# Experts' gate and up products on one Trainium2 core: weight blocks stationary instead of tokens

## The reference, cut to what matters

```
def _swiglu(h, wg, wu, wd):
    return (jax.nn.silu(h @ wg) * (h @ wu)) @ wd

top_val, top_idx = lax.top_k(logits, TOP_K)          # TOP_K = 2 of N_EXPERTS = 8
for e in range(N_EXPERTS):                           # wg, wu: 1024 x 3584, wd: 3584 x 1024
    out = out + combine[:, e:e + 1] * _swiglu(t, wg[e], wu[e], wd[e])
```

## Time and profile before

| | us |
|---|---|
| median of 3 runs | 1435.74 |
| lowest and highest | 1433.92, 1436.13 |
| the profiled execution's own time | 1435.94 |
| its span in the trace | 1434.3 |

### The profile page before, as it was taken

The page is one execution under the profiler, slowest core; times in us unless marked ns, Lnnn a source line. Parts: engine busy times, 40 slices in busy tenths (PEclk is TensorE's granted clock), DMA queues, the critical chain, the costliest instruction groups (busy, mean ns, idle before and its releaser), DMA issues.

```text
span 1434.3 us, 18278 instructions
## 1 busy us (share of the span) xinstructions
PE 1398.9 (98%) x6864; PEld 1136.0 (79%) x6864; DVE 1236.7 (86%) x1088; ACT 899.1 (63%) x793; POOL 44.7 (3%) x79
## 2 busy tenths in 40 slices
PE   5989999999999999999999999999999999999999
PEld 2765899996875888888888888888888888888886
DVE  3689778776878899999999999899999999999987
ACT  2074534443274677777777777777777777777774
POOL 0000000000000000000000000000000000000012
PEclk9999999999999999999999999999999999999999
DMA  9966669868627899999999999999999999999995
GB/s 366 415 254 216 243 220 375 295 258 333 244 110 276 300 374 374 347 394 396 339 395 396 341 397 394 390 347 393 395 340 396 396 340 397 393 382 355 393 392 150
DMA packets 195824, 484.50 MB, mean 338 GB/s; under 512 B 8926, under 2 KB 31684, under 8 KB 191684
## 3 DMA queue, kind: packets, MB, share of 16 engines
q1 hardware_dynamic: 187056, 451.17, 84.0%
q0 software_dynamic: 6480, 32.52, 6.1%
q10 hardware_dynamic: 2244, 0.22, 0.1%
HBM read 473.40 MB, written 10.49 MB: 337 GB/s over the span
## 4 chain that ended last, share of the span: by engine, by line
PE 87%; DVE 6%; DMA 3%; ACT 2%; SPq 1%; issue 1%; DVEq 0%; ACTq 0%
PE ps L1044 21%; PE ps L1046 21%; PE ps L1045 21%; PE ps L702 3%; PE ps L895 2%; PE ps L894 2%; PE ps L896 2%; PE ps L858 2%; PE ps L1087 2%; DMA split<-in_w_in 2%; PE ps L695 1%; SPq L456 1%; PE ps L902 1%; DMA arena<-in_w_ada 1%; PE ps L903 1%; PE ps L904 1%
## 5 line engine op out<-in xcount | busy, mean ns | idle before, releaser
L1962 DVE TENSOR_TENSOR split_r<-arena,split_r 128x2048 fp32r<-128x2048 f32 x336 | 763.4, 2288 | 62.2 <-ACT split_r L1372 61.7
L1372 ACT ACTIVATE split_r<-arena 128x2048 fp32r<-128x2048 f32 x334 | 640.3, 1917 | 125.3 <-PE ps L1046 122.0
L1044 PE MATMUL ps<-split_r,tokens_r 128*128 128x512 f32 x1280 | 505.4, 395 | 0.0
L1046 PE MATMUL ps<-split_r,tokens_r 128*128 128x512 f32 x1280 | 499.3, 390 | 0.0
L1045 PE MATMUL ps<-split_r,tokens_r 128*128 128x512 f32 x1280 | 498.3, 389 | 0.0
L1046 PEld LDWEIGHTS ps<-split_r,tokens_r 128*128 128x128 f32 x1280 | 240.2, 188 | 51.1
L1045 PEld LDWEIGHTS ps<-split_r,tokens_r 128*128 128x128 f32 x1280 | 240.6, 188 | 48.0
L1044 PEld LDWEIGHTS ps<-split_r,tokens_r 128*128 128x128 f32 x1280 | 240.4, 188 | 48.0 <-DVE split_r L1962 0.4
L894 PE MATMUL ps<-tokens_r,split_r 128*128 128x256 f32 x352 | 99.2, 282 | 0.2 <-DVE split_r L1802 0.2
L895 PE MATMUL ps<-hT_r,split_r 128*128 128x256 f32 x352 | 99.3, 282 | 0.0
L896 PE MATMUL ps<-tokens_r,split_r 128*128 128x256 f32 x352 | 98.6, 280 | 0.0
(11 more groups left out here) (355 smaller groups left out, 1314.1 us busy)
## 6 DMA issues: line engine op xcount, KB each, us to landing
arena<-in_moe_w_gate SPq DMA_DIRECT2D x57, 2048.0 KB, 10.5
arena<-in_moe_w_up SPq DMA_DIRECT2D x57, 2048.0 KB, 10.5
arena<-in_moe_w_down SPq DMA_DIRECT2D x56, 2048.0 KB, 10.2
arena<-in_w_ada SPq DMA_DIRECT2D x15, 1024.0 KB, 20.0
arena<-in_w_ada POOLq DMA_DIRECT2D x10, 1536.0 KB, 10.8
arena<-in_ffn_w_gate SPq DMA_DIRECT2D x11, 1024.0 KB, 5.5
arena<-in_ffn_w_up SPq DMA_DIRECT2D x11, 1024.0 KB, 10.9
arena<-in_ffn_w_down SPq DMA_DIRECT2D x11, 1024.0 KB, 14.9
```

Of the source, the lines that this page charges most:

```text
L1044: mm(out_, xh, h, start=first, stop=False, skip_group_check=True)
L1046: return mm(out_, xl, h, start=False, stop=last_, skip_group_check=True)
L1372: A(wh[:, j % SPLITS, :], piece_half(j), ACT.Copy).then_inc(sem("w_hi"), 1)
L1962: v.tensor_tensor(wl[:, j % SPLITS, :], piece_half(j), wh[:, j % SPLITS, :].bitcast(F32), ALU.subtract).then_inc(sem("w_lo"), 1)
```

## The change

Gate and up products take the form that the dense part has. In a half of a g or u piece PE now walks over the four 128-column groups f of the hidden columns and over the four blocks k of the model dimension; the weight block of 128x128 is stationary, high or low, and the tokens' 128 columns move. The result lies in the same bank as before, as four blocks of [128 hidden, 128 tokens]. Tanh and the two products of silu work on it unchanged, so `e_hid` already has the hidden columns on the partitions. The four transposes of each chunk are gone, with two waits that guarded bank 7; ACT and DVE split `e_hid` straight from SBUF, and ACT waits for `e_hid` and for PE's being done with the half at `turn_after` instead of for the transposes. PE keeps its wait for `e_hid`. Down is unchanged.

```diff
--- before.py
+++ after.py
@@ -1045,6 +1045,14 @@
                     mm(out_, xh, lo, start=False, stop=False, skip_group_check=True)
                     return mm(out_, xl, h, start=False, stop=last_, skip_group_check=True)
 
+                def columns_triple(out_, xh, xl, at, first, last_):
+
+                    b, c0 = at
+                    h, lo = wh[:, b, c0:c0 + P], wl[:, b, c0:c0 + P]
+                    mm(out_, h, xh, start=first, stop=False, skip_group_check=True)
+                    mm(out_, h, xl, start=False, stop=False, skip_group_check=True)
+                    return mm(out_, lo, xh, start=False, stop=last_, skip_group_check=True)
+
                 for j in js:
                     kind, c = pieces[j // 2]
                     half = j % 2
@@ -1067,10 +1075,12 @@
                                 if j == HP - 1 and (f, n) == (EFT // 2 - 1, 0):
                                     last.then_inc(sem("down_ps"), 1)
                     else:
-                        for k in range(KD // 2):
-                            kk = half * KD // 2 + k
-                            last = triple(ps[:, 2 * (c % 2) + (kind == "u"), :], hTh[:, kk, :], hTl[:, kk, :],
-                                          (j % SPLITS, k * EW), EW, kk == 0, kk == KD - 1)
+                        for f in range(EFT):
+                            for k in range(KD // 2):
+                                kk = half * KD // 2 + k
+                                last = columns_triple(ps[:, 2 * (c % 2) + (kind == "u"), f * P:(f + 1) * P],
+                                                      hTh[:, kk, :], hTl[:, kk, :], (j % SPLITS, k * EW + f * P),
+                                                      kk == 0 and f == 0, kk == KD - 1)
                     last.then_inc(sem("w_used"), 1)
                     if j == ROWS_AFTER:
                         slot_rows(p + 1)
@@ -1079,13 +1089,6 @@
                     if j in turn_after:
                         c = turn_after[j]
                         pe.wait_ge(sem("e_hid"), p * ECHUNKS + c + 1)
-                        if c == 1:
-                            pe.wait_ge(sem("slot_now"), p + 1)
-                        if c == 5:
-                            pe.wait_ge(sem("slot_row"), p + 1)
-                        for f in range(EFT):
-                            last = tr(ps[:, 6 + c % 2, f * P:(f + 1) * P], e_hid[:, f * P:(f + 1) * P], ident[:, :])
-                        last.then_inc(sem("fT_ps"), 1)
 
 
             pe.wait_ge(sem("consts"), 1)
@@ -1385,8 +1388,9 @@
                         act.wait_ge(sem("w_used"), p * HP + j + 1 + SPLITS)
                         A(e_tg, ps[:, 2 * (c % 2), :], ACT.Tanh, scale=0.5).then_inc(sem("e_tanh"), 1)
                     if j in turn_after:
-                        act.wait_ge(sem("fT_ps"), p * ECHUNKS + turn_after[j] + 1)
-                        A(fT_parts(turn_after[j])[0], ps[:, 6 + turn_after[j] % 2, :], ACT.Copy)\
+                        act.wait_ge(sem("e_hid"), p * ECHUNKS + turn_after[j] + 1)
+                        act.wait_ge(sem("w_used"), p * HP + j + 1 + SPLITS)
+                        A(fT_parts(turn_after[j])[0], e_hid, ACT.Copy)\
                             .then_inc(sem("fT_hi"), 1)
                     if j == SPLIT_H_AFTER and not final:
                         high_h(p + 1)
@@ -2018,7 +2022,7 @@
                         c = turn_after[j]
                         dve.wait_ge(sem("fT_hi"), p * ECHUNKS + c + 1)
                         high, low_ = fT_parts(c)
-                        v.tensor_tensor(low_, ps[:, 6 + c % 2, :], high.bitcast(F32), ALU.subtract)\
+                        v.tensor_tensor(low_, e_hid, high.bitcast(F32), ALU.subtract)\
                             .then_inc(sem("fT_lo"), 1)
                     if j == ROWS_AFTER + 2:
                         dve.wait_ge(sem("row_ps"), p + 2)
```

## The result

The changed kernel takes 2214.61 us (median of 4 runs, 2211.45 to 2215.71) where the kernel before takes 1435.86: 1.543 times as long, 95% interval 1.541 to 1.544. The profiled execution's span is 2214.0 us. The direction was right, the size was not: +779 us where +602 were forecast, and the time lies 105 us above the range's upper end.

A forecast was written before the change was run, and what follows sets the result against it. PE was taken to bound the kernel, with the weight load limiting the new gate and up matmuls: 1435.9 + 627.1 for gate and up - 25.0 for the transposes = 2038 us, range 1985 to 2110.

The forecast's parts named there:

- The load as the limit: Gate and up: weight load sets each 128-column matmul's price, 112 to 117.5 ns, taken as 115; +627 us; 81%.
- Rivals 2 and 3: Gate and up: load not overlapping the stream, whole 2597 us, 4%; load hidden in part or whole, 1478 us, 7%.
- the faster one: Gate and up: load and most overhead vanish, below 59.0 ns a matmul; at 53.3 ns the whole 1375 us; chance 2%.
- The transposes: Experts' stage on PE: dropping four transposes for each of 56 chunks, 0.447 us a chunk, saves 25.0 us.
- ACT, DVE and DMA have slack: Experts' stage: splits take ACT 1.92, DVE 2.29 us against PE's 5.5 a half; DMA needs about 227 GB/s, moved 370.
- Nothing of these can bind: Experts' stage: ACT, DVE and DMA stay within PE's time, so what they gain or lose costs nothing.
- all of it is on the path, since PE never waits: Gate and up on PE: the whole +627 us of the 10752 matmuls lengthens the run.
- PE's idling and a clock under 1.0: Experts' stage: forecast wrong if PE idles more than a few us or the clock's row shows anything under 1.0.
- Rival 1, the clock: Gate and up: half-used array lets the clock fall to 0.50, 214 ns a matmul, the whole 3103 us; chance 5%.
- The range: Whole kernel: 2002 to 2065 us for the main case, widened to 1985 to 2110.
- 22 and 32 us of widening: Range's additions: 22 us for a late split at the end of passes, 32 us for 3 ns a matmul of spacing.

The follow-up runs named there:

- a_half_loads: a_straight with 64 instead of 128 stationary columns in the second and third matmul of each triple; 1635.24 us.
- a_one_load: Changed kernel with one load of the high weight block for both token parts, a 256-column matmul replacing two; 1669.76 us looped, 1627.76 us with PE's passes written out.
- a_hint: Changed kernel with a prefetch hint for the backward branch of PE's loop; 2032.15 us.
- a_straight: Changed kernel with PE's seven passes written out instead of a loop, other engines still looping; 2002.49 us.
- b_two_passes: Kernel before with two passes in each turn of PE's loop, 1084 matmuls in the body instead of 542; 1445.80 us.
- a_edge_at_down: Changed kernel with PE's loop beginning right ahead of the first down piece, order of the work kept; 2024.82 us.
- a_wide: Changed kernel with 14 added 512-column float32 products behind the first half piece of each turn of PE's loop; 2155.86 us.

## Why the prediction was wrong

- *The load as the limit*: right. 111.7 ns measured in the stream, inside 111.6 to 117.5; my 115 lay 3.3 ns, or 35 us, too high. The float32 rows of 64 columns were the better guide than the nearest fp32r row, whose stream is the limit there. a_half_loads and a_one_load confirm the term from two sides. Rivals 2 and 3 and the faster one fall with it.
- *The transposes*: right, 25.0 us by the rows, 23.8 by the run.
- *ACT, DVE and DMA have slack*: right; none appears as a releaser of PE.
- *"Nothing of these can bind", and the sum's "all of it is on the path, since PE never waits"*: this is the step that failed. I costed each of the 10752 matmuls on the array and none as an instruction. The body of PE's loop grew from 542 to about 1520 matmuls, each with its load. At the return to its start PE then stood idle for code, 4.25 us each time; a_hint, a_straight and b_two_passes show that it was the branch and the body's length. The trace of before had a row that I did not ask about: 29 packets of code in the whole run and none between 600 and 1300 us, that is, a loop whose body did not have to be transferred again. The prediction named PE's idling and a clock under 1.0 as signs of being wrong, and both came, but its sum had no term for either.
- *Rival 1, the clock*: its trigger and its recovery were taken as one thing. The row that spoke against it was right in what it showed: a half-used array at full clock keeps it, as a_straight does for 1500 us. What it could not show is that the same stream, once at 0.50, does not bring it back, where 512-column products do in some 5 us. I gave the rival 5% as a loss over the whole stage (3103 us); it came as 68.3 us at the lower level in each of six passes, for a price of 31 us each. The two missing terms are 25.5 and 187 us, together the 212 us by which 2214.6 lies above 2002.5.
- *The range*: its own terms, 22 and 32 us of widening, give 2065 + 54 = 2119 and 2002 - 32 = 1970, not 2110 and 1985. 2214.6 lies outside either.

The Trainium skill (page "TensorE: Matmul & The Clock Gate", section on HAM oscillation) says that an idle gap between two bursts of matmuls makes the next one start at the lower clock. These runs agree for most gaps, and add how much hangs on what follows: 68.3 us of low clock behind a gap for one form, 3.4 to 6.8 us for the other. The same page's 81 ns for pairs of a load and a 128-column matmul (section "Back-to-back issue gap"), which the prediction had beside rival 3, does not hold for fp32r here: 111.7 ns.

## What to carry to other kernels

With full 128-column stationary blocks in fp32r, a moving operand of 128 columns costs nearly as much as one of 256 (111.7 against 117.5 ns); turning a product round to save a transpose paid here neither in the loop nor written out, because its moving side became narrow. Count what a change does to the length of a loop's body on each engine, and look at the instruction queue's row. A body whose code is transferred anew in each turn can cost idle time at each return; writing it out took all of that away, a hint five of six, another place for the branch over half. Put whatever idle time must remain ahead of wide products, not ahead of narrow ones.

## What the runs showed of the hardware that was not expected

- One return to the start of a long body costs PE two idle times in the changed kernel, 1.4 to 2.0 and 1.8 to 3.5 us, each ending 2.2 to 3.0 us behind the start of a packet of code; ahead of 512-column products there is one. Why the second packet starts only some 6 us behind the first (901.1 and 907.4 us) was not tried.
- An idle time of 1.4 us was enough to put the clock down at one return of the changed kernel, and one of 1.75 us was not at one return of a_edge_at_down. In the changed kernel, a_hint and a_wide the clock fell between 0.6 us ahead of and 1.9 us behind the end of a return's first idle time, so the second did not start it.
- A stream of fp32r matmuls with 128 moving columns runs at 111.7 ns at a granted clock of 1.00 and at 213 ns at 0.50: the load slows with the clock (0.19 us at full, 0.33 us at low clock in the records).
